# Expert weights in tile pairs: products of 512 columns, three 1 MB pieces a pair, one pipeline across the items

## What is computed

```python
def _swiglu(h, wg, wu, wd):
    a = jax.nn.silu(jnp.einsum('bld,df->blf', h, wg)) * jnp.einsum('bld,df->blf', h, wu)
    return jnp.einsum('blf,fd->bld', a, wd)

def _moe(h, router, wg, wu, wd):
    logits = jnp.einsum('bld,de->ble', h, router).astype(jnp.float32)
    top_v, top_i = lax.top_k(logits, TOP_K)
    gates = jax.nn.softmax(top_v, axis=-1)
    dense_gate = jnp.sum(jax.nn.one_hot(top_i, N_EXPERTS, dtype=jnp.float32) * gates[..., None], axis=-2)
    out = jnp.zeros_like(h)
    for e in range(N_EXPERTS):
        out = out + dense_gate[..., e:e + 1].astype(h.dtype) * _swiglu(h, wg[e], wu[e], wd[e])
    return out
```

## Time and profile before

| | |
|---|---|
| three runs, median (lowest, highest) | 1893.72 us (1891.28 to 1897.6) |
| the profiled execution | 1892.12 us |
| its span, first to last instruction | 1890.1 us |
| TensorE, VectorE, ScalarE busy | 92%, 72%, 58% of the span |
| moved, all queues | 494.22 MB, 261 GB/s over the span |
| weight slabs of the experts | 224 transfers of 1536 KB |
| mean granted clock | 0.95 |

### The profile page before, as it was taken

One profiled execution on the slowest core, in us unless ns is written; L12 is line 12 of the kernel. 1 busy time (PEld: TensorE's weight loads), 2 busy tenths in 40 slices (PEclk: granted clock), 3 DMA queues, 4 the chain that ended last, 5 costly groups with the idle time before them and its releaser, 6 DMA issues.

```text
span 1890.1 us, 33664 instructions
## 1 busy us (share of the span) xinstructions
PE 1731.4 (92%) x11984; PEld 1536.9 (81%) x11984; DVE 1356.2 (72%) x2228; ACT 1091.5 (58%) x1837; POOL 39.4 (2%) x47
## 2 busy tenths in 40 slices
PE   6997888999989887767999999999999999999995
PEld 3884457999978654556999999999999999999995
DVE  4477345454455754357889889898898988988985
ACT  4453324444344532245777777777777777777772
POOL 0000100000000000000000000000000000000000
PEclk8998898999989997688999999999999999999998
DMA  9651362445436314037999999999999999999993
GB/s 385 219 199 45 135 266 90 156 165 186 160 112 236 136 45 164 1 159 268 363 360 365 355 347 379 359 357 365 353 363 359 346 380 360 360 359 348 370 358 124
DMA packets 52272, 494.22 MB, mean 261 GB/s; under 512 B 6256, under 2 KB 6560, under 8 KB 11120
## 3 DMA queue, kind: packets, MB, share of 16 engines
q1 hardware_dynamic: 48000, 479.59, 67.3%
q0 software_dynamic: 3840, 12.57, 1.8%
q10 hardware_dynamic: 368, 1.19, 0.2%
HBM read 484.97 MB, written 8.35 MB: 261 GB/s over the span
## 4 chain that ended last, share of the span: by engine, by line
PE 86%; DVE 8%; ACT 3%; DMA 2%; issue 2%; DVEq 0%; SPq 0%; ACTq 0%; POOLq 0%
PE bank L1019 17%; PE bank L1004 11%; PE bank L1006 11%; PE bank L1005 11%; PE bank L582 7%; PE bank L584 7%; PE bank L583 7%; PE bank L618 3%; PE bank L1012 1%; PE bank L590 1%; PE bank L865 1%; PE bank L778 1%; PE bank L843 1%; PE bank L597 1%; PE bank L839 1%
## 5 line engine op out<-in xcount | busy, mean ns | idle before, releaser
L1983 DVE TENSOR_TENSOR w_lo<-xring,w_hi 128x1024 fp32r<-128x1024 f32 x448 | 528.7, 1221 | 94.3 <-ACT w_hi L1335 94.3
L1004 PE MATMUL bank<-w_hi,hg_hi 128*128 128x256 f32 x1792 | 510.2, 285 | 5.6 <-DVE w_lo L1983 2.9
L1006 PE MATMUL bank<-w_hi,hg_lo 128*128 128x256 f32 x1792 | 507.9, 283 | 0.0
L1005 PE MATMUL bank<-w_lo,hg_hi 128*128 128x256 f32 x1792 | 507.7, 283 | 0.0
L1335 ACT ACTIVATE w_hi<-xring 128x1024 fp32r<-128x1024 f32 x448 | 449.7, 1060 | 0.0
L1004 PEld LDWEIGHTS bank<-w_hi,hg_hi 128*128 128x128 f32 x1792 | 342.1, 191 | 17.9 <-DVE w_lo L1983 4.7
L1005 PEld LDWEIGHTS bank<-w_lo,hg_hi 128*128 128x128 f32 x1792 | 342.1, 191 | 7.5
L1006 PEld LDWEIGHTS bank<-w_hi,hg_lo 128*128 128x128 f32 x1792 | 342.3, 191 | 0.0
L1983 DVE TENSOR_TENSOR wd_lo<-xring,wd_hi 128x1024 fp32r<-128x1024 f32 x224 | 273.0, 1219 | 0.0
L1338 ACT ACTIVATE wd_hi<-xring 128x1024 fp32r<-128x1024 f32 x224 | 236.5, 1056 | 2.1 <-PEq L973 2.1
L1351 ACT ACTIVATE sgX<-bank 128x128 f32<-128x128 f32 x224 | 62.2, 278 | 252.2 <-PE bank L1006 252.2
(11 more groups left out here) (305 smaller groups left out, 2613.5 us busy)
## 6 DMA issues: line engine op xcount, KB each, us to landing
xring<-w_moe SPq DMA_DIRECT2D x224, 1536.0 KB, 8.6
ring<-w_ada SPq DMA_DIRECT2D x32, 1536.0 KB, 7.7
ring<-w_win SPq DMA_DIRECT2D x22, 1024.0 KB, 6.6
ring<-w_up SPq DMA_DIRECT2D x22, 1024.0 KB, 4.8
ring<-w_down SPq DMA_DIRECT2D x8, 1408.0 KB, 5.9
ring<-w_wo SPq DMA_DIRECT2D x8, 1024.0 KB, 6.3
ring<-w_wqb SPq DMA_DIRECT2D x2, 1152.0 KB, 8.6
ring<-w_wkvb SPq DMA_DIRECT2D x2, 1024.0 KB, 5.5
```

The lines of the kernel that those rows point to most:

```text
L1004: mm(banks[j][:, 0:256], hg_hi[:, k], w_hi[:, j % 2, cols], start=k == 0, stop=False)
L1005: mm(banks[j][:, 0:256], hg_hi[:, k], w_lo[:, j % 2, cols], start=False, stop=False)
L1006: last = mm(banks[j][:, 0:256], hg_lo[:, k], w_hi[:, j % 2, cols], start=False, stop=k == KD - 1)
L1983: v.tensor_tensor(lo, xring[:, s + D * p:s + D * p + D], hi.bitcast(F32), ALU.subtract).then_inc(sem("lo_done"), 1)
```

## The change

Two neighbouring tiles become a pair. A product of `gate_up` takes the 256 gate and up columns of both tiles, 512 moving columns, into one bank; a pair has 24 of them in two halves of 12 (blocks 0 to 3, then 4 to 7). A pair's weights come in three pieces of 1 MB, each with 1024 columns of either tile: blocks 0 to 3, blocks 4 to 7, the down part. Each piece is loaded, rounded and subtracted by itself, in one instruction per engine. In DRAM a piece is 256 rows of 4 KB, where a slab was 128 rows of 12 KB; the layout in DRAM is as before. `xring` has room for two pairs, `w_hi` and `w_lo` for one buffer per half, `wd_hi` and `wd_lo` for two pairs. TensorE runs the first half of pair r, `turn` of r - 1, the second half of r, `down` of r - 1. At the end of an item the next item's first pair takes its place in this order, on every engine.

```diff
@@ -43,7 +43,7 @@
+PAIRS, PIECE = NFX // 2, 2 * D
...
@@ -395,17 +395,18 @@
-        xring = sb("xring", XSLOT * SLOTW)
+        xring = sb("xring", 6 * PIECE)
+        xpiece = xring[:, :].rearrange("p (r m n) -> p r m n", r=2, m=3)
...
-        wd_hi = tiles(sb("wd_hi", 4 * D, F32R)[:, :], 4)
-        wd_lo = tiles(sb("wd_lo", 4 * D, F32R)[:, :], 4)
+        wd_hi = tiles(sb("wd_hi", 4 * D, F32R)[:, :], 2)
+        wd_lo = tiles(sb("wd_lo", 4 * D, F32R)[:, :], 2)
...
-        at_hi = tiles(sb("at_hi", 4 * 128, F32R)[:, :], 4)
-        at_lo = tiles(sb("at_lo", 4 * 128, F32R)[:, :], 4)
-        sgX = tiles(sb("sgX", 2 * 128)[:, :], 2)
-        aX = tiles(sb("aX", 2 * 128)[:, :], 2)
+        at_hi = tiles(sb("at_hi", 4 * 128, F32R)[:, :], 2)
+        at_lo = tiles(sb("at_lo", 4 * 128, F32R)[:, :], 2)
+        sgX = tiles(sb("sgX", 2 * 256)[:, :], 2)
+        aX = tiles(sb("aX", 2 * 256)[:, :], 2)
...
@@ -444,7 +445,7 @@
+        piece_full = [[sem("piece_full%d%d" % (r, p)) for p in range(3)] for r in range(2)]
...
@@ -524,28 +525,33 @@
-                    sp.wait_ge(sem("lo_done"), i * (3 * NFX) + q * (3 * XSLOT) + (3 * j + 3))
-                    sp.dma_start(xring[:, j * SLOTW:(j + 1) * SLOTW],
-                                 w_moe[bass.ds(base + q * XSLOT + j, 1)].rearrange("a p n -> (a p) n")
-                                 ).then_inc(xslot_full[j], 16)
+            sp.sem_inc(sem("lo_done"), 6)
+            def load_pair(r, index):
+                for p in range(3):
+                    if index is not None:
+                        i, q, base = index
+                        sp.wait_ge(sem("lo_done"), i * (3 * PAIRS) + q * 6 + (3 * r + p + 1))
+                        first = bass.ds(base + q * 4 + 2 * r, 2)
+                    else:
+                        first = slice(2 * r, 2 * r + 2)
+                    sp.dma_start(xpiece[:, r, p].rearrange("p (u n) -> p u n", u=2),
+                                 w_moe[first, :, D * p:D * (p + 1)].rearrange("u p n -> p u n")
+                                 ).then_inc(piece_full[r][p], 16)
+            for r in range(2):
+                load_pair(r, None)
+            with sp.Fori(1, PAIRS // 2) as q:
+                for r in range(2):
+                    load_pair(r, (0, q, 0))
...
+                with sp.Fori(0, PAIRS // 2) as q:
+                    for r in range(2):
+                        load_pair(r, (i, q, e * NFX))
...
@@ -989,67 +996,80 @@
+            def gate_up(i, q, r, half):
+                pe.wait_ge(sem("lo_done"), i * (3 * PAIRS) + q * 6 + (3 * r + 7 + half))
+                if half == 0:
+                    pe.wait_ge(sem("a_ready"), i * PAIRS + q * 2 + (r + 1))
+                for k in range(4 * half, 4 * half + 4):
+                    hi, lo = (tiles(w[:, half], 2)[:, :, 256 * (k % 4):256 * (k % 4) + 256] for w in (w_hi, w_lo))
+                    mm(banks[r % 2][:, :], hg_hi[:, k], hi, start=k == 0, stop=False)
+                    mm(banks[r % 2][:, :], hg_hi[:, k], lo, start=False, stop=False)
+                    last = mm(banks[r % 2][:, :], hg_lo[:, k], hi, start=False, stop=k == KD - 1)
+                last.then_inc(sem("gate_up_done"), 1)
+            def first_gate_up(i, half):
+                pe.wait_ge(sem("hg_split"), i * 2 + (half + 1))
+                gate_up(i, 0, 0, half)
+            def turn(i, q, r):
+                pe.wait_ge(sem("a_ready"), i * PAIRS + q * 2 + (r + 3))
+                pe.wait_ge(sem("at_split"), i * PAIRS + q * 2 + (r + 1))
+                for u in range(2):
+                    last = nc.tensor.transpose(banks[2 + r % 2][:, 128 * u:128 * u + 128],
+                                               aX[:, r % 2, 128 * u:128 * u + 128], ident)
+                last.then_inc(sem("turned"), 1)
+            def down(i, q, r, first=False):
+                if first:
+                    pe.wait_ge(sem("y_lo_ready"), i + 1)
+                    pe.wait_ge(sem("y_hi_ready"), i + 1)
+                pe.wait_ge(sem("at_split"), i * PAIRS + q * 2 + (r + 3))
+                pe.wait_ge(sem("lo_done"), i * (3 * PAIRS) + q * 6 + (3 * r + 9))
+                for t in range(2):
...
+                            c = D * t + 512 * u
+                            last = mm(banks[4 + u][:, :], a[:, r % 2, 128 * t:128 * t + 128], w[:, r % 2, c:c + 512],
+                                      start=first and t == 0 and n == 0, stop=False, skip_group_check=True)
+                last.then_inc(sem("down_done"), 1)
+            def pair(i, q, r, first=False):
+                gate_up(i, q, r, 0)
+                turn(i, q, r - 1)
+                gate_up(i, q, r, 1)
+                down(i, q, r - 1, first)
+            def item(i, more):
+                pair(i, 0, 1, True)
+                if more:
+                    invert(i + 1)
+                with pe.Fori(1, PAIRS // 2 - 1) as q:
+                    pair(i, q, 0)
+                    pair(i, q, 1)
+                q = PAIRS // 2 - 1
+                pair(i, q, 0)
+                if more:
+                    for half in range(2):
+                        gather(i + 1, half)
+                pair(i, q, 1)
+                if more:
+                    first_gate_up(i + 1, 0)
+                turn(i, q, 1)
+                if more:
+                    first_gate_up(i + 1, 1)
+                down(i, q, 1)
...
+            for half in range(2):
+                first_gate_up(0, half)
...
@@ -1327,56 +1347,67 @@
+            def round_piece(i, q, r, p):
+                act.wait_ge(piece_full[r % 2][p], i * (8 * PAIRS) + q * 16 + 16 * (r // 2 + 1))
+                if p < 2:
+                    act.wait_ge(sem("gate_up_done"), i * (2 * PAIRS) + q * 4 + (2 * r + p + 1))
+                else:
+                    act.wait_ge(sem("down_done"), i * PAIRS + q * 2 + (r + 1))
+                A(w_hi[:, p] if p < 2 else wd_hi[:, r % 2], xpiece[:, r % 2, p], ACT.Copy).then_inc(sem("hi_done"), 1)
+            def round_tokens(i, b):
+                act.wait_ge(sem("gathered"), i * 2 + (b + 1))
+                act.wait_ge(sem("gate_up_done"), i * (2 * PAIRS) + (b + 1))
+                A(hg_hi[:, 4 * b:4 * b + 4], banks[6 + b][:, :].rearrange("p (k n) -> p k n", k=4), ACT.Copy
+                  ).then_inc(sem("hg_rounded"), 1)
+            def silu(i, q, r):
+                act.wait_ge(sem("gate_up_done"), i * (2 * PAIRS) + q * 4 + (2 * r + 4))
+                act.wait_ge(sem("a_ready"), i * PAIRS + q * 2 + (r + 1))
+                A(sgX[:, r % 2].rearrange("p (u n) -> p u n", u=2),
+                  banks[r % 2][:, :].rearrange("p (u c n) -> p u c n", u=2, c=2)[:, :, 0], ACT.Silu).then_inc(sem("silu_x"), 1)
+            def round_hidden(i, q, r):
+                act.wait_ge(sem("turned"), i * PAIRS + q * 2 + (r + 1))
+                act.wait_ge(sem("down_done"), i * PAIRS + q * 2 + (r + 1))
+                A(at_hi[:, r % 2], banks[2 + r % 2][:, 0:256], ACT.Copy).then_inc(sem("at_rounded"), 1)
+            def pair(i, q, r):
+                round_piece(i, q, r, 2)
+                round_hidden(i, q, r - 1)
+                round_piece(i, q, r + 1, 0)
+                silu(i, q, r)
+                round_piece(i, q, r + 1, 1)
...
+                pair(i, 0, 1)
+                with act.Fori(1, PAIRS // 2 - 1) as q:
+                    for r in range(2):
+                        pair(i, q, r)
+                q = PAIRS // 2 - 1
+                pair(i, q, 0)
+                round_piece(i, q, 1, 2)
+                round_hidden(i, q, 0)
...
+                    round_tokens(i + 1, 0)
+                    round_piece(i + 1, 0, 0, 0)
+                silu(i, q, 1)
...
+                    round_tokens(i + 1, 1)
+                    round_piece(i + 1, 0, 0, 1)
+                    round_piece(i + 1, 0, 0, 2)
+                round_hidden(i, q, 1)
+                if more:
+                    round_piece(i + 1, 0, 1, 0)
+                    silu(i + 1, 0, 0)
+                    round_piece(i + 1, 0, 1, 1)
+                act.wait_ge(sem("down_done"), i * PAIRS + (PAIRS + 2))
...
@@ -1973,73 +2008,84 @@
+            def piece_rest(i, q, r, p):
+                dve.wait_ge(sem("hi_done"), i * (3 * PAIRS) + q * 6 + (3 * r + p + 1))
+                hi, lo = (w_hi[:, p], w_lo[:, p]) if p < 2 else (wd_hi[:, r % 2], wd_lo[:, r % 2])
+                v.tensor_tensor(lo, xpiece[:, r % 2, p], hi.bitcast(F32), ALU.subtract).then_inc(sem("lo_done"), 1)
+            def tokens_rest(i, b):
+                dve.wait_ge(sem("hg_rounded"), i * 2 + (b + 1))
+                v.tensor_tensor(hg_lo[:, 4 * b:4 * b + 4], banks[6 + b][:, :].rearrange("p (k n) -> p k n", k=4),
+                                hg_hi[:, 4 * b:4 * b + 4].bitcast(F32), ALU.subtract).then_inc(sem("hg_split"), 1)
+            def multiply(i, q, r):
+                dve.wait_ge(sem("silu_x"), i * PAIRS + q * 2 + (r + 1))
+                v.tensor_tensor(aX[:, r % 2].rearrange("p (u n) -> p u n", u=2),
```

(40 more changed lines are left out.)

171 lines of the change are left out of this document (17 added, 154 removed).

## The result

The changed kernel takes **1859.45 us** (median of four runs, 1858.49 to 1859.75), the kernel before 1892.65 us (1891.28 to 1897.6) on the same chip: a ratio of 0.9821, 95% interval 0.9809 to 0.9833. It is 33.2 us faster; forecast were 26.7. The profiled execution took 1858.49 us, its span is 1856.4.

What follows compares the result with a forecast made beforehand. TensorE's own issue was taken to bound the expert stage; -24.7 (steady part) - 1 (seams) - 2 (start) + 1 (end) = -26.7 us from 1892.1 gave 1865.4, and 1867 us as the runs' median, range 1850 to 1884.

Steps and rivals of the forecast that it cites:

- What bounds: Expert stage: TensorE's own issue sets the pace, VectorE a tenth behind, nobody waiting for a weight transfer.
- The steady part: Gate and up products: 24 of 512 columns replace 48 of 256, saving 0.22 us a pair, 24.7 us over 112 pairs.
- the row with the same width: Down products of 512 columns, same types, a weight load each: step 0.230 us, taken for the new gate and up products.
- another width: Dense layer's 288-column products, every 0.1329 us: the same overhead at 512 columns gives 0.2263, saving 0.31 a pair, 35 us.
- The other engines: VectorE and ScalarE in a pair: hidden behind TensorE at 7.7 and 6.6 us of 8.52; first half has 0.8 us to spare.
- The transfers: Expert weight stream: 369 GB/s needed in an 8.52 us pair, more room available, 4 KB rows costed at nothing.
- memory rival: Expert stage already bound by memory at 360 GB/s, only the edges' -2 us stays: 1892 us; chance 0.10.
- rows' rival: Weight pieces: 4 KB rows slow the stream to 346 GB/s, +39 us, 1933 us; chance 0.07.
- The seams: Between items: 2.4 us against some 2.6 before, second half's piece about 0.8 us late; 7 seams, -1 us in all.
- The start: Start of expert stage: index read 1.1 us earlier, first half needing only half the tokens saves 0.9: -2 us.
- The end: Last hidden tile: its chain runs bare before its down products, 2.8 us covered by previous down products: +1 us.

Runs made afterwards that it cites:

- experiment 1: Changed kernel with each 512-column gate and up product cut into two of 256 columns, all else kept: 1886.96 us, ratio to the kernel before 0.9966.
- experiment 5: Changed kernel with a pair's two transposes moved ahead of its first half of gate and up products: 1856.55 us, ratio to the kernel before 0.9821.
- experiment 11: Changed kernel with a third of the products left out and weight pieces in 8 KB rows: 1745.77 us, ratio to the kernel before 0.9235.
- experiments 6 and 7: Changed kernel with VectorE's choice for the item after next moved behind the second half's first piece (1856.11 us), or behind the first pair's at_lo (1854.38 us).

## Why the prediction was right, point by point

**What bounds.** TensorE, as read. The chain, the granted clock of 1.00 and ScalarE's waits for TensorE say so, and experiment 1 shows it by giving the width back.

**The steady part: right in kind, a third too small.** This is the mis-sized term. Forecast were 24.7 us; 112 x (8.747 - 8.413) = 37.4 came. The term is the step of the 24 wide products, 0.230 us in the forecast. The forecast took the step of the row with the same width, 0.230, over the row with another width that gave 0.2263; 0.2267 was measured. "Same width, same types" was not the whole likeness: the down products stood in sixes behind a transpose and 256-column products, and experiments 5 and 1 show 512-column products stepping more slowly at first in such places. At 0.2267 the 24 products save 0.30 a pair. The last 0.03 fits the count of such places: before, 512-column products began anew twice a pair, in each tile's six down products; now the 36 of a pair are broken once, at the transposes, and experiment 1, whose pair also has one such place, keeps the 0.033. That is argued from the counts and was not tested by itself; the forecast's working, with the down products unchanged, had no place for it. The Trainium skill ("TensorE: Matmul & The Clock Gate", Back-to-back issue gap) has 2.5 ns on top of the columns, which made 7 us of it in the prediction; the section gives that gap for a product by itself, not for a stream with a weight load for each, which is what runs here. The trace has 13 ns on top at 256, 288 and 512 columns alike, 0.2267 against 0.2133, and the saving of the 24 products is the 24 times 13 ns a pair that this says.

**The other engines.** 2.29 and 1.91 us a piece against 2.29 and 1.95; 0.76 us to spare for the first half against 0.8. VectorE 90%. The one thing not foreseen, ScalarE waiting 0.53 us a pair for the down products to leave wd_hi (50.9 us in all), is hidden.

**The transfers.** 368 to 382 GB/s against 365 to 370, as the pair is shorter; no wait for them; 8 KB rows no better. The memory rival and the rows' rival fall as forecast. The reason given, that the share is a queue that holds work, is borne out by 386 GB/s in a stretch of experiment 5 and by 422 in experiment 11, where only the rows and TensorE's load differ. The Trainium skill's figure of about 358 GB/s as the limit of one core's HBM ("DMA: Bandwidth & Descriptors", Specifications), on which that rival could rest, is passed in every one of these stretches; the section gets it by dividing a stack's 716 GB/s between two cores, and here one core streams alone.

**The seams.** Forecast 2.4 against 2.6, measured 2.8 against 2.7; the stall for w_lo is 0.64 where 0.8 was worked out, and its cause is the one named, the scaling and the choice ahead of the piece, as experiments 6 and 7 show. So +1 instead of -1 us in all.

**The start: wrong in sign.** Forecast -2. The index is indeed read 2.75 us after the permutation's choice where it was 3.96, but the first product came only 0.3 us earlier, since the stage itself began 1.5 us later in this execution. And then the half buffers, which the forecast had cleared for the steady part alone, bite once: TensorE begins the stage at a granted clock of 0.50, 1.2 GHz (steps of 0.43 us until 870.2), so the first half leaves its buffer late, nothing older is left to compute meanwhile, and TensorE waits 1.61 us for the second pair's w_lo. The old kernel had such a wait too, of 0.73 us at its third tile:

```profile
873.72 0.39 PE L1004 MATMUL bank<-w_hi,hg_hi 128*128 128x256 f32 x1 [0.73 <-DVE w_lo L1983]
```

From the first product to the second inversion the new kernel needs 18.6 us for 60 products of 512 columns, which at their step with the transposes are 14.0; the old one 16.0 us for 96 products of 256 and six of 512, 13.2. The loss is 4.6 us where it was 2.8. Of the 1.8 us more, 0.9 is the longer wait; the other 0.9 is about what the lower clock cost more, which lasted from 864.9 to 870.2 here and from 865.2 to 869.1 in the old kernel (why it rose later was not tried). That makes +1.8 less the 0.3, or +1.5, and 3.5 us off the forecast.

**The end.** +1 forecast; TensorE waits 1.0 us for at_lo ahead of the last down products.

Together: -37.4 + 1 + 1.5 + 1 = -33.9, against -33.8 from the start of the span to the last scaling (1866.5 and 1832.7). The errors of the steady part (12.7 us) and of seams and start (5.5 us) are of opposite sign, so that the total was closer than its largest term; that part is luck.

## What to carry to other kernels

When an operation's price is taken from a row, look at what stands ahead of it as well as at its shape: two rows of equal width can differ by 1.5% by their place, one behind shorter operations and one in a run of its like, and the better estimate here was the constant on top of the columns that two other widths agreed on. Where a delay on a helper engine shows as a stall, moving the instruction that seems to cause it moves the stall, until it goes where that engine has time to spare. And a limit that is never reached, like the 4 KB rows', costs nothing today and decides the next change.
